# Expert blocks of a two-layer diffusion backbone: the order of turn, gate arithmetic, gathers and scatters

## The reference

```python
h2 = modulate(rms_norm(x, norm_ffn[l]), sh2, sc2)
x = x + g2 * moe_ffn(h2, router_w, router_b, moe_w_gate[l], ...)
# in moe_ffn: each token takes 2 of 16 experts, with weights gates[:, e]
out = swiglu(xs, ws_gate, ws_up, ws_down)
for e in range(N_EXPERTS):
    out = out + gates[:, e:e + 1] * swiglu(xs, w_gate[e], w_up[e], w_down[e])
# swiglu(x, wg, wu, wd) = (silu(x @ wg) * (x @ wu)) @ wd
```

## Time and profile before

| what | us |
|---|---|
| median of 3 runs | 1554.87 |
| lowest and highest of them | 1551.24, 1561.84 |
| the profiled execution | 1557.56 |
| its span in the profile | 1555.7 |

### The profile page before, as it was taken

One profiled execution on the slowest core, in us unless ns is written; L12 is line 12 of the kernel. 1 busy time (PEld: TensorE's weight loads), 2 busy tenths in 40 slices (PEclk: granted clock), 3 DMA queues, 4 the chain that ended last, 5 costly groups with the idle time before them and its releaser, 6 DMA issues.

```text
span 1555.7 us, 25318 instructions
## 1 busy us (share of the span) xinstructions
PE 1496.0 (96%) x9438; PEld 996.8 (64%) x9438; DVE 894.1 (57%) x1852; ACT 395.7 (25%) x886; POOL 311.0 (20%) x464
## 2 busy tenths in 40 slices
PE   5999999999999999999999999999999999999995
PEld 4655445766665577677777554555766666678883
DVE  2323523467676667667666853533667766765556
ACT  1322113455554420000000322113455541000001
POOL 0111101000000000555453111201000000265532
PEclk9999999999999999999999999999999999999998
DMA  9642112640011296699998853213811026489994
GB/s 360 208 149 108 55 51 65 218 150 21 22 41 42 75 344 252 222 332 351 355 339 304 290 190 111 106 51 100 275 58 42 15 79 221 163 316 339 339 355 176
DMA packets 104936, 283.49 MB, mean 182 GB/s; under 512 B 20404, under 2 KB 34268, under 8 KB 95080
## 3 DMA queue, kind: packets, MB, share of 16 engines
q1 hardware_dynamic: 91728, 261.03, 46.9%
q0 software_dynamic: 12528, 21.03, 3.7%
q10 hardware_dynamic: 584, 0.14, 0.0%
HBM read 262.52 MB, written 38.53 MB: 194 GB/s over the span
## 4 chain that ended last, share of the span: by engine, by line
PE 75%; DVE 8%; DMA 7%; issue 6%; POOL 3%; ACT 1%; SPq 0%; POOLq 0%; DVEq 0%; ACTq 0%
PE S L1309 18%; PE B L1478 9%; PE S L1398 8%; PE S L1690 7%; PE PT L1419 6%; PE B L1455 6%; DMA arena<-h,arena 4%; PE S L1701 4%; PE B L1333 3%; DMA arena<-in_w_mod 2%; PE B L1205 2%; PE S L1333 2%; DVE arena L2325 2%; POOL arena L1867 1%; PE S L1569 1%
## 5 line engine op out<-in xcount | busy, mean ns | idle before, releaser
L1309 PE MATMUL S<-arena 128*128 128x512 f32 (+3 forms) x768 | 295.8, 535 | 2.6 <-ACT arena L974 2.6
L1690 PEld LDWEIGHTS S<-arena 128*128 128x128 f32 x2304 | 263.6, 192 | 31.2 <-issue 31.2
L1690 PE MATMUL S<-arena 128*128 128x128 f32 x2304 | 266.0, 275 | 11.4 <-DVE arena L2603 8.2
L1309 PEld LDWEIGHTS S<-arena 128*128 128x128 f32 x768 | 139.8, 190 | 122.6 <-issue 102.1
L1081 ACT ACTIVATE arena<-S,nmax 128x768 f32<-128x768 f32 (+1 forms) x200 | 154.8, 778 | 145.4 <-DVE nmax L2203 120.9
L1867 POOL DMA_INDIRECT arena<-h,arena x144 | 154.5, 1073 | 172.2 <-issue 104.8
L2203 DVE TENSOR_REDUCE nmax<-S 128x1 f32<-128x768 f32 (+1 forms) x168 | 133.2, 826 | 70.6 <-PE S L1398 60.6
L1478 PE MATMUL B<-arena 128*128 128x512 f32 x320 | 153.7, 602 | 0.6 <-DVE arena L2261 0.5
L1398 PE MATMUL S<-arena 64*128 64x256 f32 (+5 forms) x624 | 135.2, 473 | 2.2 <-ACT arena L1081 2.2
L1701 PE MATMUL S<-arena 128*128 128x512 f32 x288 | 129.6, 592 | 0.0
L1419 PEld LDWEIGHTS PT<-cst,arena 128*128 128x128 f32 x768 | 86.9, 141 | 65.3 <-issue 51.8
(11 more groups left out here) (326 smaller groups left out, 1675.6 us busy)
## 6 DMA issues: line engine op xcount, KB each, us to landing
arena<-in_w_mod SPq DMA_DIRECT2D x24, 2048.0 KB, 10.1
arena<-in_moe_w_gate SPq DMA_DIRECT2D x36, 1024.0 KB
arena<-in_moe_w_up SPq DMA_DIRECT2D x36, 1024.0 KB
arena<-in_moe_w_down SPq DMA_DIRECT2D x36, 1024.0 KB
arena<-in_w_in SPq DMA_DIRECT2D x6, 2048.0 KB, 11.4
arena<-y SPq DMA_DIRECT2D x20, 512.0 KB, 5.9
arena<-mod SPq DMA_DIRECT2D x16, 512.0 KB, 6.8
arena<-in_tokens SPq DMA_DIRECT2D x12, 512.0 KB, 9.6
```

What stands on the lines that cost most here:

```text
L1309: mm = pe.matmul(ubank[u % 4][:, c0:PANEL_W[p]], hT[:, k, t * P:(t + 1) * P], panel[p][:, k, c0:], start=k == 0, stop=k == KT - 1)
L1690: mm = pe.matmul(to, wgu[b][:, w, k * DE + h * P:k * DE + (h + 1) * P], XT[b][:, k, :], start=k == 0, stop=k == KT - 1)
```

## The change

In VectorE's `e_block`, gate_mul of the running block stands ahead of the turn of the next, and row_gate of the block before it, which stood in `e_out` behind both, stands ahead of gate_mul. In GpSimd's loop the gather stands ahead of the scatter. Both hold for both layers, but for row_gate, which layer 1 doesn't have. e_out is L2601 and row_gate's instruction still L2592 after the change.

```diff
--- before.py
+++ after.py
@@ -1921,8 +1921,8 @@
                     late_zeros(b)
                 with pool.Fori(2, pairs) as i:
                     for b in range(2):
+                        e_gather(2 * i + b, b)
                         e_scatter(2 * i + b - 4, b, b)
-                        e_gather(2 * i + b, b)
                 for b in range(2):
                     e_scatter(2 * pairs_2 + b, b, b)
                 if l == 0:
@@ -2592,8 +2592,6 @@
                     dve.scalar_tensor_tensor(gate, g2[:, 1, :], is_ctx[:, span(blk, 1)], g2[:, 0, :], ALU.mult, ALU.add).then_inc(s["v_gate"], 1)
 
                 def e_out(blk, u, b, first):
-                    if l == 0:
-                        row_gate(blk, not first or b == 1)
                     dve.wait_ge(s["e_d"], ge(blk) + 1)
                     if not first:
 
@@ -2606,9 +2604,11 @@
                 def e_block(blk, u, b, more, first, out_first):
 
                     last = not first or b
+                    if l == 0 and last:
+                        row_gate(blk - 1, not first)
+                    gate_mul("e_", ge(blk), gex[b], (S0, S1)[b][:, 0:DE])
                     if more:
                         x_turn(blk + 1, u + b, 1 - b)
-                    gate_mul("e_", ge(blk), gex[b], (S0, S1)[b][:, 0:DE])
                     if last:
                         e_out(blk - 1, u + b - 1, 1 - b, out_first)
                     e_up_mul(ge(blk), b)
```

## The result

Median 1559.84 us (1555.73 to 1563.09, 20 runs) against 1554.11 us for the kernel before (1550.22 to 1561.84, 20 runs): ratio 1.0041, 95% interval 1.0031 to 1.0050. A second set of runs of the same two kernels gave 1557.06 against 1552.81, ratio 1.0018 [1.0005, 1.0031]. The forecast was 1547 us, a gain of 0.5%; both medians lie above its whole range. The profiled execution took 1559.32 us (span 1557.5).

A forecast was written before the change was run, and what follows sets the result against it. TensorE, busy 96% of the span, was taken as the bound, so only its standstill could be won: layer 0 -7.9 us and layer 1 -0.3, together -8.2, from the median of 1554.87 to 1547 us; range 1541 to 1556.

The forecast's parts named there:

- The 8.2 us of standstill: Layer 0, gate product of block 2 to up product of block 19: TensorE stands still 8.2 of 195.15 us, all to go.
- I take the median and say 1547: The total: the 8.2 us gain taken from the runs' median of 1554.87 us, not from the profiled execution's 1557.56.
- a loss of 0.3: Layer 0's opening blocks: gate product of block 1 1.7 us late, that of block 2 at 663.8 instead of 663.51.
- The gather loop: Layer 0, two blocks a round: gathers described ahead of scatters cut it to 14.2 to 15.5 us, against TensorE's 21.16.
- the scatter behind it: GpSimd's scatter, described after the gather, leaves some 5 to 7 us later; yb is reused 13 us on; cost 0.
- row_gate: Layer 0, 1.29 us per block: moved to where VectorE waits for exp, cost 0, taking 1.5 us out of VectorE's chain.
- the landings in layer 0: gate_mul ahead of the turn takes the gather's landing out of gate_mul's way; VectorE lost 30.9 us to landings.
- Rival 2: The DMA engines become the bound in layer 0: a pair takes 21.8 us, about 1552 in all; chance 0.10.
- In layer 1 the same start costs about 0.5 us: Layer 1's opening, block 1's turn behind gate_mul(0): about 0.5 us lost, a 0.73 us wait before gate(2) gone, gain 0.3.
- The slack is 0.2 to 0.5 us; I take no stall: Steady blocks, T the gate product's start: e_out at T+8.7 to T+8.9, TensorE free by T+10.35, before T+10.58.
- rival 1: VectorE's chain (turn, e_out, next gate) becomes the bound; each 0.1 us beyond T+10.58 costs 3 us; chance 0.20, slower 0.08.
- Rival 4: GpSimd's fourth gather describe holds VectorE's gate_mul by its whole length, 1 us: 11 us slower, 1566; chance 0.02.

## Why the prediction was wrong

- *The 8.2 us of standstill.* Its mechanism was right and the changed kernel has none of it, but the size was that of one execution. The step that failed is "I take the median and say 1547": the term was measured in an execution 2.7 us over the median, whose surplus was partly this very standstill, and was then taken from the median whole. Two more profiles of before hold 2.3 us in place of 7.9, and those at gate(2), in a wait and a half clock that the prediction priced as a loss of 0.3. (3.57 and 3.44 make 7.0, not 7.1, so 8.3 us of standstill in that profile; it changes nothing.)
- *The gather loop, the scatter behind it, row_gate, the landings in layer 0.* Right: in the changed kernel no wait for e_out from gate(2) on, GpSimd waits for turns, 10.58 in every block. What was wrong is that both halves were needed; either alone frees layer 0's loop. Rival 2 did not bind: from 664.0 to 840.1 the changed kernel moved 357 GB/s at a DMA share of 0.95.
- *"In layer 1 the same start costs about 0.5 us".* This is the step that turned the sign. It took exp at its steady T+3.8, while before's own profile had exp(0) 5.93 us behind gate(0). It costs 0.5 to 4.9 us, and up to 2.3 of half clock: 6.7, 2.4 and 6.4 in three profiles, against openings of 20.0.
- *"The slack is 0.2 to 0.5 us; I take no stall"* (and rival 1). In layer 0 this held in every profile of the changed kernel; in steady blocks e_out starts at T+8.8 to T+8.9, as forecast. In layer 1, once late, a block takes 10.7: 1.3 us in all. Rival 1 named the place, but as a state that binds or doesn't; it is one that is entered.
- *Rival 4* put the describe on the start of gate_mul. L2324 took 0.39 us at 1453.99 beside a describe of 1453.29 to 1454.28 in the second profile of the changed kernel, 0.29 alone; it was not held by its length. The Trainium skill (SBUF — State Buffer, "SBUF: two separate sides") has whichever starts first keep the shared ports for its whole instruction, where VectorE's is in a 2-port mode or has two inputs in SBUF; L2324 has one input, and no run shows its mode. If it is in that mode, the trace disagrees beside the describe. Beside a memset (1371.32, 0.97 us), L2324 started at 1371.22 and took 1.22, as if it had waited for it.
- *Net.* By the profiles: -2.3 + 2.4 to 6.7 + 1.3, so 1.4 to 5.7 us slower. The medians say 5.7 and 4.25.

What stays open: why the signal of gate(0) comes late in twelve of the 20 profiles, and why all five of the kernels with gathers first and VectorE's new order throughout are among them (exp(0) at 5.2 to 8.2 us; with both down weights later the signal itself was only 0.3 us late) while the three others with gate_mul first are not (what they have over 3.9 us is the clock). By the medians these three pay little there. Chance isn't excluded: before itself had it in two of three profiles, and the run with scatters first and a delay had 8.1. The load burst behind the rows of block 0 isn't the whole reason: of the four runs that changed it one had the signal 0.3 us late, the three others 2.4 to 3.7 us.

## What to carry to other kernels

Before a wait is priced from one profile, look at whether the time of that execution is typical, and take two or three profiles of the kernel before if the term depends on how fast DMAs land. When an instruction is moved behind another, price it by the first and last rounds of the loop with their own rows, not by the steady one: the order of an opening block can be chosen by itself. Here the old one was the better in layer 1's first block, the new one in layer 0's. Where a chain is left a few tenths of slack, ask what it takes once it is late, and test it by being late on purpose.

## What the runs showed of the hardware

- exp(0) of layer 1 starts 3.8 to 8.2 us behind the gate product that it reads, in one and the same kernel (5.2 to 8.2). The trace names no engine or DMA as the releaser ("remote"), but has the increment of the gate product's semaphore 0.02 to 0.03 us before exp(0): the signal is late, not ScalarE. In the five profiles with the latest signals TensorE pauses too, and goes on with the increment. No instruction packet moved between gate(0) and exp(0) in any of the 20 profiles: the DMA queues from 1344 to 1365 of the changed kernel are

```profile
q1 hardware_dynamic: 866, 3.95, 50.0%
q0 software_dynamic: 576, 0.81, 13.5%
```

- With the turn first and the down weights later, gate(1) lasted from 1357.46 to the start of the down product at 1364.94, 7.5 us for 3.6, with the DMA share at 1.03 and 1.10 in the two stretches shown:

```profile
1358.00:1360.00 2.00, 1.35 (x6) 0.84 (x6) 1.45 (x2) 0.00 (x0) 1.70 (x2) 1.00 1.03 380
1360.00:1362.00 2.00, 1.60 (x11) 1.45 (x11) 0.00 (x0) 0.00 (x0) 1.39 (x3) 1.00 1.10 396
```

The granted clock was 1.00, no semaphore is named, and TensorE was busy 1.35 and 1.60 of 2 us. Whether its instructions, its operands or the records were late isn't shown, nor that the load was the cause: in gate(0) of the changed kernel, at a share of 1.03 (1352 to 1355), the products came evenly. In steady blocks at a share of 0.94 nothing like it shows.
